# Turning the second layer's input by VectorE squares and a DRAM exchange, instead of half by TensorE

## What is computed

```
def _layernorm(x, g, b):
    mu = xf.mean(-1, keepdims=True)
    var = jnp.mean(jnp.square(xf - mu), -1, keepdims=True)
    y = (xf - mu) * lax.rsqrt(var + LN_EPS) * g + b

def _layer(x, mem, ...):
    (r_q, r_k, r_v, a_cq, ..., l_x, ..., c_q, z) = _split_cols(x @ w_in, IN_SPLITS)
    ...
    k, v = jnp.split(mem @ w_mem_kv, 2, axis=-1)     # does not need x
    ...
    y = y.astype(x.dtype) @ w_out
    return _layernorm(DEEPNORM_ALPHA * x + y, ln_g, ln_b)
```

## Time and profile before

| | us |
|---|---|
| median of 3 runs | 889.2 (888.85 to 889.35) |
| the profiled execution | 888.95 |
| its span, first to last instruction | 887.1 |
| layer two begins on TensorE, about | 440.2 |
| `lx0` begins on TensorE | 485.5 |

### The profile page before, as it was taken

The page is one execution under the profiler, slowest core; times in us unless marked ns, Lnnn a source line. Parts: engine busy times, 40 slices in busy tenths (PEclk is TensorE's granted clock), DMA queues, the critical chain, the costliest instruction groups (busy, mean ns, idle before and its releaser), DMA issues.

```text
span 887.1 us, 13174 instructions
## 1 busy us (share of the span) xinstructions
PE 881.4 (99%) x4516; PEld 757.0 (85%) x4516; DVE 662.7 (75%) x1326; ACT 488.6 (55%) x914; POOL 17.8 (2%) x18
## 2 busy tenths in 40 slices
PE   9999999999999999999999999999999999999997
PEld 8888998888888888888888889888888888888896
DVE  6869697878594677766679787978777878786765
ACT  6655785545455346544477566745355453565641
POOL 0000000000000000000000000000000001000001
PEclk9999999999999999999999999999999999999999
DMA  9796487547669688666677876885485874967822
GB/s 357 289 332 203 136 273 263 170 139 225 214 220 321 214 242 262 201 195 196 191 239 231 295 254 179 263 261 168 140 276 144 280 237 155 291 219 250 329 86 95
DMA packets 72402, 200.33 MB, mean 226 GB/s; under 512 B 9608, under 2 KB 24208, under 8 KB 71696
## 3 DMA queue, kind: packets, MB, share of 16 engines
q1 hardware_dynamic: 71760, 198.44, 68.8%
q10 hardware_dynamic: 576, 1.05, 0.4%
HBM read 183.43 MB, written 16.00 MB: 225 GB/s over the span
## 4 chain that ended last, share of the span: by engine, by line
PE 98%; issue 1%; ACT 0%; POOL 0%; DVE 0%; POOLq 0%; ACTq 0%; DVEq 0%
PE acc L1347 24%; PE acc L1348 24%; PE acc L1351 24%; PE acc L1362 10%; PE acc L1368 5%; PE work L1136 1%; PE work L1135 1%; PE work L1134 1%; PE work L1253 1%; PE work L1252 1%; PE work L1118 0%; PE work L1275 0%; PE work L1264 0%; PE work L1192 0%; PE work L1186 0%
## 5 line engine op out<-in xcount | busy, mean ns | idle before, releaser
L1434 DVE TENSOR_TENSOR lo<-raw,hi 128x512 fp32r<-128x512 f32 (+2 forms) x607 | 387.5, 656 | 181.6 <-ACT hi L1093 174.2
L1093 ACT ACTIVATE hi<-raw 128x512 fp32r<-128x512 f32 (+2 forms) x607 | 356.0, 604 | 297.3 <-PE acc L1351 234.7
L1347 PE MATMUL acc<-hi,xx 128*128 128x512 f32 (+2 forms) x768 | 285.5, 374 | 0.0
L1348 PE MATMUL acc<-hi,xx 128*128 128x512 f32 (+2 forms) x768 | 283.6, 372 | 0.0
L1351 PE MATMUL acc<-lo,xx 128*128 128x512 f32 (+2 forms) x768 | 223.0, 372 | 0.0
L1348 PEld LDWEIGHTS acc<-hi,xx 128*128 128x128 f32 x768 | 144.6, 188 | 23.6
L1347 PEld LDWEIGHTS acc<-hi,xx 128*128 128x128 f32 x768 | 144.6, 188 | 23.6
L1351 PEld LDWEIGHTS acc<-lo,xx 128*128 128x128 f32 x768 | 140.4, 188 | 24.6
L1362 PE MATMUL acc<-xx,hi 128*128 128x512 f32 x384 | 96.0, 392 | 0.0
L1362 PEld LDWEIGHTS acc<-xx,hi 128*128 128x128 f32 x384 | 69.3, 189 | 12.5
L1368 PEld LDWEIGHTS acc<-xx,lo 128*128 128x128 f32 x384 | 52.4, 190 | 3.7
(11 more groups left out here) (348 smaller groups left out, 965.5 us busy)
## 6 DMA issues: line engine op xcount, KB each, us to landing
raw<-in_w SPq DMA_DIRECT2D x263, 512.0 KB, 4.3
B<-turn SPq DMA_DIRECT2D x80, 128.0 KB, 4.2
raw<-in_w SPq DMA_DIRECT2D x26, 256.0 KB, 2.7
turn<-B SPq DMA_DIRECT2D x12, 512.0 KB, 5.6
raw<-in_w SPq DMA_DIRECT2D x16, 328.0 KB, 3.2
turn<-Y SPq DMA_DIRECT2D x8, 512.0 KB, 5.4
Y<-in_wuq SPq DMA_DIRECT2D x2, 1152.0 KB, 9.5
Y<-in_x_t SPq DMA_DIRECT2D x4, 512.0 KB, 8.7
```

What stands on the lines that cost most here:

```text
L1093: act.activation(place(l, t, hi), raw[:, s, (t % 2) * w:(t % 2 + 1) * w], ACT.Copy)\
L1347: pe.matmul(o, ah[:, q], hi[:, s, 0:w], start=k == 0, stop=False, skip_group_check=name == "memv")
L1348: pe.matmul(o, al[:, q], hi[:, s, 0:w], start=False, stop=False, skip_group_check=name == "memv")
L1434: dve.tensor_tensor(place(l, t, lo), raw[:, s, (t % 2) * w:(t % 2 + 1) * w], place(l, t, hi).bitcast(F32), ALU.subtract).then_inc(lo_done. ...
```

## The change

TensorE's four `xT` jobs go. All four column blocks are turned by `square_x`, in slots 10, 11, 13 and 14, and the blocks are normalised in order 0 to 7. The exchange now has two groups of two column blocks (group 0: j = 0 to 3, group 1: j = 4 to 7). Each group is written out by one transfer of 1 MB in rows of 8 KB and read back in four pieces of 256 KB, each of 32 partitions in rows of 2 KB, into Y instead of B[2] and B[0]. `x_squares` lies over B[4] to B[7]. The write of group 0 stands after pair 10, that of group 1 after pair 12; the read-backs stand after pairs 13 and 15 and each waits for its own write. Since Y now holds the turned input, the loads of `wukv` and `wuq` after pair 22 wait for `x_lo` 7.

```
-for _j in range(4):
-    _put(LATER_PE, 18 + _j // 2 * 4, "xT", _j)
...
-    _put(LATER_ACT, 8 + _j, "normalise", (4, 5, 6, 7, 0, 1, 2, 3)[_j])
-    _put(LATER_ACT, (23, 24, 27, 28, 29, 30, 32, 33)[_j], "x_hi", _j)
+    _put(LATER_ACT, 8 + _j, "normalise", _j)
+    _put(LATER_ACT, (24, 25, 26, 27, 29, 30, 31, 32)[_j], "x_hi", _j)
...
-_put(LATER_DVE, 11, "square_x", 2)
-_put(LATER_DVE, 13, "square_x", 3)
+for _cb in range(4):
+    _put(LATER_DVE, (10, 11, 13, 14)[_cb], "square_x", _cb)
 for _j in range(8):
-    _put(LATER_DVE, (24, 26, 28, 30, 32, 33, 35, 37)[_j], "x_lo", _j)
+    _put(LATER_DVE, (25, 27, 28, 30, 32, 33, 35, 37)[_j], "x_lo", _j)
...
-                        if l == 0:
-                            sp.wait_ge(x_lo.sem, x_lo.at(0, 7))
-                        else:
-                            sp.wait_ge(y_lo.sem, y_lo.at(l - 1, 7))
+                        sp.wait_ge(x_lo.sem, x_lo.at(l, 7))
...
-                    if l and m in (10, 11):
-                        sp.wait_ge(x_squared.sem, m - 9)
-                        sp.dma_start(a["x_turn"][m - 10], x_squares[m - 10]).then_inc(x_turn_out.sem, 16)
-                    if l and m in (14, 15):
-                        sp.wait_ge(x_turn_out.sem, 2 * 16)
+                    if l and m in (10, 12):
+                        g = (m - 10) // 2
+                        sp.wait_ge(x_squared.sem, 2 * g + 2)
+                        sp.dma_start(a["x_turn"][g], x_squares[:, g]).then_inc(x_turn_out[g].sem, 16)
+                    if l and m in (13, 15):
+                        g = (m - 13) // 2
+                        sp.wait_ge(x_turn_out[g].sem, 16)
+                        sp.wait_ge(y_lo.sem, y_lo.at(l - 1, 7))
                         for b in range(4):
-                            sp.dma_start(x_turned[m - 14][b * 32:(b + 1) * 32, :].rearrange("c (a n) -> c a n", a=4),
-                                         a["x_turn"][m - 14, :, b * 256:(b + 1) * 256].rearrange("(a c) n -> c a n", a=4))\
-                              .then_inc(xT_in[m - 12].sem, 16)
+                            sp.dma_start(x_turned[b * 32:(b + 1) * 32, g].rearrange("c (a n) -> c a n", a=4),
+                                         a["x_turn"][g, :, b * 512:(b + 1) * 512].rearrange("(a c) n -> c a n", a=4))\
+                              .then_inc(xT_in[g].sem, 16)
...
-                    if j < 4:
-                        wait_job(act, l, ("xT", j))
-                    else:
-                        act.wait_ge(xT_in[j // 2].sem, 16 + 4 * 16)
+                    act.wait_ge(xT_in[j // 4].sem, 16 + 4 * 16)
...
                 def square_x(cb):
-                    dve.wait_ge(normed.sem, 2 * cb - 2)
+                    dve.wait_ge(normed.sem, 2 * cb + 2)
```

More of the change, by code:

```diff
@@ L351, in both, with both_x @@
             return sb(f"B{i}", [P, size]), same_place
-        row_of = {i: both(i, 4 * SEQ) for i in (1, 2, 4, 5, 6, 7, 8, 9)}
+        turned_place = {}
+        def both_x(i, size):
+            if i == 4:
+                with nc.sbuf_tensor("x_squares", [P, 2, 8 * SEQ], F32) as x_place:
+                    turned_place["x"] = x_place
+            return both(i, size)
+        row_of = {i: both_x(i, 4 * SEQ) for i in (1, 2, 4, 5, 6, 7, 8, 9)}
         row_of[0] = both(0, NT * HEADS * (HD + 1))
@@ L545, in build_trunk @@
         scaled, copied = signal("scaled", 0), signal("copied", 0)
-        x_squared, x_turn_out = signal("x_squared", 0), signal("x_turn_out", 0, step=16)
+        x_squared, x_turn_out = signal("x_squared", 0), [signal(f"x_turn_out{g}", 0, step=16) for g in range(2)]
         stored = signal("stored", 0, step=16)
@@ L1139, in both @@
                     return tuple(at(x) for x in parts)
-                def xT(j):
-                    pe.wait_ge(ident_in.sem, 16)
-                    pe.wait_ge(normed.sem, 2 * (j // 2) + 6)
-                    o = take("xT", j)
-                    for kk in range(2):
-                        for i in range(NT):
-                            m = turn(o[:, kk * 256 + i * P:kk * 256 + (i + 1) * P],
-                                     X[:, i, (2 * j + kk) * P:(2 * j + kk + 1) * P])
-                    m.then_inc(job_done.sem, 1)
                 def mem_scores(h):
@@ L1288, in ret_out @@
                     m.then_inc(job_done.sem, 1)
-                steps = {"xT": xT, "mem_scores": mem_scores, "mem_out": mem_out,
+                steps = {"mem_scores": mem_scores, "mem_out": mem_out,
                          "ml_fold": ml_fold, "ml_q": ml_q,
```

25 lines of the change are left out of this document (9 added, 16 removed).

## The result

The changed kernel takes 901.1 us (median of 4 runs, 899.23 to 902.08) where the kernel before takes 889.3 beside it. The ratio is 1.0132, with a 95% interval of 1.012 to 1.0143: 11.9 us slower. The forecast was 891.0 in a range up to 893.4. The direction was right and the size was missed by 10 us, far outside the range. The profiled execution of the changed kernel took 899.23, the fastest of the four, with a span of 897.4.

The account below looks back on a forecast made before the run. TensorE bounds the kernel, busy 881.4 of 887.1 us. Removing transposes saves 1.74 us, but group 0's late read-back makes the change 1.8 us slower net: 889.2 + 1.8 = 891.0 us, range 888.0 to 893.4.

Parts of the forecast that it names:

- Removal, 1.74 us: TensorE's row before `lx0`: sixteen transposes, two lots of 0.87 us, leave it and save 1.74 us.
- Squares free: Slots 10 to 14: two more column blocks cost VectorE two lots of 1.30 us, covered by its lead; fourth ends 458.0.
- Write 0 lands at 461.7: SyncE's queue: group 0's 1 MB write, issued at about 454.65, lands at about 461.7.
- The engines have to move 4.2 MB ... I take 468: DMA queue from about 456: pairs 10 to 13 and both writes move before group 0's read-back, until 466.8 to 469.1.
- S: Time when group 0's read-back is complete: forecast 472.8, ends 469.7 and 474.9; full gain only at or below 469.2.
- Price of a piece, 1.2 us: Group 0's read-back: each 256 KB piece taken at 1.2 us, four at 4.8 us.
- Who waits for S: ScalarE stands 4.6 us at `x_hi` 0; VectorE ends `x_lo` 7 at S + 22.9, holding the fourth pair of `lx0`.
- What is queued behind the pieces: Transfers after group 0's read-back: group 1 and the rest taken as in time, costing nothing.
- main case: Group 0 complete at S = 472.8 (471.7 to 474), fourth pair of `lx0` late, net cost 1.8 us; chance 0.52.
- rival 3: Both groups late: group 1 takes until 482 or more, ScalarE stands at `x_hi` 4; net about +4, 893.2; chance 0.17.
- TensorE before `lx0`: Sign: TensorE standing before slots 25 to 31 would mean rival 3 or a longer S.
- `wukv` and `wuq`: Weight loads waiting for `x_lo` 7, needed by TensorE's pair 46, 47: 0 to 0.6 us over the edge, taken as nothing.

Follow-up runs that it names:

- full list issued in one go: Only transfers, no kernel computation: six weight pairs, two writes and two groups read back in 32-partition pieces, issued without a pause; 26.7 us a round.
- the list at the kernel's times of issue: Only transfers: the same pairs, writes and read-backs, each issued when the changed kernel issues it; first group complete after 21.5, 21.2 and 22.9 us (kernel 23.3).
- one-read kernel: The changed kernel with each group written by four transfers from 32 partitions and read back by one into 128 partitions; 893.2 us, ratio 1.0044.
- tuned version: Changed kernel with four writes and one read a group, group 0's read ahead of the second write, `x_hi` 4 to 7 later, `wukv` earlier; 888.9 us, 0.9995.
- crossed order: The changed kernel with the four read-back pieces of a group issued in the order 0, 2, 1, 3; 898.1 us, ratio 1.0095.

## Why the prediction was wrong in size

- **Removal, 1.74 us**: right. Measured by itself 1.4 us (0.9 to 2.5).
- **Squares free**: right for the engines. The fourth ends at 458.0, as worked out, and no other engine waits for it. But SyncE's queue does: pair 11 was issued at 458.62 (before: 456.75), and the second write at 460.19 (before: 457.12). The next but one point shows what that did.
- **Write 0 lands at 461.7**: 461.1.
- **"The engines have to move 4.2 MB ... I take 468"**: wrong by 2.9 us. The first piece landed at 472.1, which with 1.2 us a piece was to be 469.2. The step assumed an unbroken stream from 456 at the rate of the earlier trace rows. The second write is only issued at 460.19, after the squares, and the stretch moved 267 GB/s at a share of 0.86: (319 - 267) x 8 us = 0.42 MB were left over, some 1.3 us. The rest is that pieces begin while pair 13 is still under way (it took 9.9 us and landed at 472.1 too). The step also misread its upper rate: the fastest slice in the earlier trace rows is 357 GB/s, not 389. With 357 the 4.2 MB take 11.8 us, to 467.8, so that the early end of S is 470.7 instead of 469.7, and 468 was the fast end and not a middle.
- **Price of a piece, 1.2 us**: right alone (1.15), in the full list issued in one go (1.2) and for three of the kernel's pieces (1.2 to 1.4 apart); the fourth landed 2.8 behind the third. 4.8 us became 6.6 with the first. What holds the fourth piece back isn't shown: with one group in the queue it doesn't happen (1.4), with equal rounds of the list at the kernel's times of issue it happened in one of three, and with pieces for all partitions in the kernel the fourth was late too (2.2 us behind the third, the others 0.7 to 0.9 apart). The estimate by the Trainium skill, SBUF — State Buffer, "Door 1: The DMA port swizzle" (8 ports at 27.2 GB/s each, 218 GB/s together, 1.2 us for 256 KB), is what the quiet queue shows with 1.15. That the ports are also what slows the whole queue to 226 GB/s isn't shown. The Trainium skill, DMA: Bandwidth & Descriptors, "Rules for kernel authors", names 128 partitions beside the large transfer in its row on the highest bandwidth. The prediction took over only the size. The pieces for 32 partitions gained nothing by longer rows (4.23 us for 512 KB, 6.75 for 1 MB, each with its wait), and one read of 1 MB into 128 partitions cost 2.35 us in the list against their 5.35, so this trace agrees with the row as a whole.
- **Who waits for S**: right. ScalarE stood at `x_hi` 0, and with S = 472.7 the one-read kernel ended `x_lo` 7 at S + 23.2.
- **What is queued behind the pieces**: the step that failed most. The main case let `x_lo` 7 end at S + 22.9 and took all else, group 1 above all, to be in time; that term stood at nothing. Only rival 3 (chance 0.17) looked at group 1. Its mechanism is what happened: `x_lo` 7 ends 15.7 us behind group 1, and with its 482 that is 497.7, 3.8 beyond the 493.9 of before, its "about +4". But group 1 came at 487.5, and 487.5 + 15.7 = 503.2 is the fourth pair as measured. So rival 3 had the right path with group 1 placed 5.5 us too early. Adding up the list with the prices above gives 10.7 us for the two groups.
- **TensorE before `lx0`**: the text said that a stand there would mean rival 3 or a longer S. It was both. The hi of slot 25 ends at S + 1.6 as forecast, and TensorE ran out of work at 474.3, so each microsecond of S beyond 472.7 stands in its row in full. The forecast lay just at that edge and didn't say so. For the time of the kernel this did not decide, since group 1 came later still.
- **The clock**: 1.4 us in slot 25 that no term had. It added nothing to the result, because it is over before the stand for group 1.
- **`wukv` and `wuq`**: no stand over 0.3 us in the change, within the 0 to 0.6. In other versions TensorE stood there up to 2.5 us (0.3 with one read, 1.4 in the tuned version, 1.5 with pieces into all partitions, 2.5 in crossed order), so the term was not understood; in the change it came out right by luck.

In sum, at the fourth pair: the forecast had 495.7. With S 4.7 us late its own law gives 500.4. Group 1 takes it to 503.2, 2.8 more, and 0.9 comes later in the span. That is 888.95 + 1.8 + 4.7 + 2.8 + 0.9 = 899.2, the profiled execution. Both delays come from the same queue, two groups of pieces for 32 partitions with writes and weights between. The runs show this as a whole: other destination 7.9 us less, one group only 1.0 us over the kernel before, no writes 3.5 us less. S alone would have made 895.7 on the median's scale, already outside the range; group 1 at 487.5 would have made 898.5 whatever S was, as long as S + 22.9 stayed below 503.2.

## What to carry to other kernels

Price a transfer at its place: list what the queue holds from the last idle moment on, with each one's cost and time of issue, and read off not only when it lands but when the weights behind it do. Here a read-back into 32 partitions held up what was queued with it; the exchange on the writing side, with one read into all partitions as far ahead in the queue as the data allow, took the loss away, though it brought no gain over the kernel before. When a stream of inputs comes in groups, write down the law for each group (here S + 23.2 and group 1 + 15.7) and take the latest: a law for the first group alone says nothing about the second. Losses ahead of a later wait don't add to it.

## What the runs showed of the hardware that was not expected

- DMA engines can be at a share of 1.06 and move 226 GB/s, or 419 just before at 1.01. In the same six microseconds it was 210 GB/s with pieces for 32 partitions and 398 with the same bytes for all partitions. Pieces that write to 32 partitions cost 5.35 us per MB in the list, those to all partitions 3.0 ((22.0 - 10.3 - 5.7) / 2), one read with long rows 2.35.
- The other side is cheaper than the 5.1 us between pairs of four pieces into 32 partitions: four writes that read from 32 partitions each cost 4.3 us between pairs against 2.8 for one write (alone 5.9 against 3.9), yet with them and one read the kernel is 8 us faster than the change.
- The same list issued in one go delivers its first group after 18.8 us, spread over the kernel's times after 21 to 23, and rounds of it differ by 2 us. The runs of one kernel with such pieces spread from 892.0 to 897.4, those of the kernel before by 0.7 to 3 us, those of the tuned version, which has none, by 3.
- After a stand of 4.8 us TensorE was granted the lower level of its clock for about 3 us (with eight small pieces after 3.8 us, with contiguous pieces after 3.6); after 3.1 us in the crossed order and after stands of 1.0 to 1.4 us in the change it kept the full one.
